# A two-block transformer kernel: the conditioning product goes to VectorE, token-major weights are joined to 512 and 384 columns, and the row-maximum scores use the whole array

## The reference, cut to what matters

```python
def hybrid_layer(x, ...):                                    # block 1
    proj = rmsnorm(x, norm1_w) @ w_in                        # 1024 x 3088
    ... y_a, y_b, y_c ...
    x = x + jnp.concatenate([y_a, y_b, y_c], -1) @ w_out
    h2 = rmsnorm(x, norm2_w)
    x = x + jnp.square(jax.nn.relu(h2 @ w_ff1)) @ w_ff2      # 1024 x 4096, 4096 x 1024

    for l in range(DEPTH_2):                                 # block 2, two layers
        mod = silu_c @ w_ada[l] + b_ada[l]                   # the conditioning product, 1024 x 6144
        sh_a, sc_a, g_a, sh_f, sc_f, g_f = jnp.split(mod[:, None, :], 6, axis=-1)
        mc = jnp.split(silu_cc @ w_ada[l][:, :n_c] + b_ada[l][:n_c], n_c // d)
        hx = rmsnorm_2(x) * (1 + sc_a) + sh_a
        ux = hx @ w_in[l]
        ...
        x = x + g_a * (jnp.concatenate([fx, ax, rx], -1) @ w_out[l])
        x = x + g_f * swiglu(rmsnorm_2(x) * (1 + sc_f) + sh_f, w_gate[l], w_up[l], w_down[l])
```

## Time and profile before

| | us |
|---|---|
| median of 3 runs | 2642.99 |
| lowest and highest | 2638.92, 2647.79 |
| span of the profiled execution | 2634.4 |
| time of the profiled execution around its span | not given; the median stands 8.6 above the span |
| PE busy in the span | 2471.9 |
| DVE, ACT, POOL busy | 870.6, 781.6, 798.1 |
| mean granted TensorE clock | 0.963 |

### The profile page before, as it was taken

The page is one execution under the profiler, slowest core; times in us unless marked ns, Lnnn a source line. Parts: engine busy times, 40 slices in busy tenths (PEclk is TensorE's granted clock), DMA queues, the critical chain, the costliest instruction groups (busy, mean ns, idle before and its releaser), DMA issues.

```text
span 2634.4 us, 37662 instructions
## 1 busy us (share of the span) xinstructions
PE 2471.9 (94%) x16546; PEld 1889.5 (72%) x16546; DVE 870.6 (33%) x1277; ACT 781.6 (30%) x980; POOL 798.1 (30%) x280
## 2 busy tenths in 40 slices
PE   7997888999999999979899999999799989999998
PEld 5874566777777787446788888888668446788886
DVE  3004236255346432842411111112442663311113
ACT  4222233122224412533322121122332543322222
POOL 3232133333333221502222222222222332344442
PEclk9997899999999999979999999999999889999999
DMA  4431023444443101002111111111210102222221
GB/s 175 172 139 33 18 84 140 162 182 152 176 160 146 48 25 47 2 3 83 62 49 64 64 65 64 64 56 49 74 49 9 47 3 103 83 103 96 96 88 56
DMA packets 41571, 216.66 MB, mean 82 GB/s; under 512 B 4088, under 2 KB 13064, under 8 KB 18112
## 3 DMA queue, kind: packets, MB, share of 16 engines
q1 hardware_dynamic: 38184, 207.87, 21.5%
...
...
## 4 chain that ended last, share of the span: by engine, by line
PE 76%; DVE 6%; ACT 3%; issue 1%; POOL 0%; DMA 0%; DVEq 0%; ACTq 0%; POOLq 0%
PE PS L676 60%; PE PS L679 3%; PE PS L1114 2%; PE PS L1147 2%; DVE s_states L1513 1%; PE PS L762 1%; DVE a_lo L599 1%; DVE tmp L606 1%; PE PS L1818 1%; PE PS L1913 1%; PE PS L1710 1%; PE PS L1164 1%; DVE x L619 1%; PE PS L1126 1%; ACT w_hi L805 1%
## 5 line engine op out<-in xcount | busy, mean ns | idle before, releaser
L2041 POOL TENSOR_TENSOR w_lo<-raw,w_hi 128x2048 fp32r<-128x2048 f32 (+3 forms) x164 | 660.8, 4034 | 1522.8 <-ACT w_hi L805 1522.8
L676 PE MATMUL PS<-a_hi,w_hi 128*128 128x512 f32 (+1 forms) x2104 | 700.1, 374 | 49.0 <-DVE a_lo L599 24.1
L676 PE MATMUL PS<-a_lo,w_hi 128*128 128x512 f32 (+1 forms) x2104 | 684.0, 366 | 0.0
L676 PE MATMUL PS<-a_hi,w_lo 128*128 128x512 f32 (+1 forms) x2104 | 680.0, 364 | 0.0
L676 PEld LDWEIGHTS PS<-a_hi,w_hi 128*128 128x128 f32 x2104 | 361.6, 190 | 149.4 <-issue 67.8
L676 PEld LDWEIGHTS PS<-a_hi,w_lo 128*128 128x128 f32 x2104 | 363.1, 190 | 68.0
L676 PEld LDWEIGHTS PS<-a_lo,w_hi 128*128 128x128 f32 x2104 | 362.5, 190 | 62.6 <-issue 1.5
L805 ACT ACTIVATE w_hi<-raw 128x2048 fp32r<-128x2048 f32 (+2 forms) x146 | 270.4, 1852 | 398.8 <-PE PS L676 185.4
L676 PE MATMUL PS<-hid_hi,w_hi 128*128 128x512 f32 (+1 forms) x784 | 260.4, 369 | 2.1 <-issue 2.1
L676 PE MATMUL PS<-hid_lo,w_hi 128*128 128x512 f32 (+1 forms) x784 | 260.8, 369 | 0.0
L676 PE MATMUL PS<-hid_hi,w_lo 128*128 128x512 f32 (+1 forms) x784 | 258.6, 366 | 0.0
...
## 6 DMA issues: line engine op xcount, KB each, us to landing
...
```

The source lines that it names most:

```text
L676: mm = p.matmul(ps[:, dst], wv[:, k, idx * P:(idx + 1) * P], av[:, k, dst], start=first, stop=last)
L2041: pool.tensor_tensor(w_lo[:, m % 2, ks, 0:ncol], raw[:, i % 3, ks, 0:ncol], w_hi[:, m % 2, ks, 0:ncol].bitcast(F32), ALU.subtract).then_in ...
```

## The change

Five things change.

1. The conditioning product. Its weights are laid transposed (`lay_turned`): on each partition one output feature, with 1024 products along the row. DVE multiplies and sums with `tensor_tensor_reduce`, which adds the bias as the start value and writes one column of `mods`: 2 x 128 features of a panel, for 2 rows of conditioning in the first 32 panels (4 instructions) and for one row in the last 16 (2 instructions). PE and ACT take no part in it any more. `c` is activated by ACT as 16 rows, stored to DRAM, and loaded back onto all partitions (`c_wide`, later `c_late`).
2. The placing of the ada panels: 12 in `in1` (after its second panel and each later one), 4 in `out1`, 8 in `ff1_0`, 8 in `ff1_1`, 12 in `ff2_0_0`, 4 in `ff2_0_1`.
3. "relu2": ACT takes ReLU from PSUM, squares and rounds; DVE only makes `hid_lo`.
4. Token-major weights are joined: two matrices of 512 columns in block 1 and one of 384 columns in each layer, each loaded as two halves of 512 rows. They stand last in their phase. A panel in memory is now contiguous in its slot (`compact`).
5. Row maxima: `k_round` holds the keys with the other head's 64 rows set to 0, so that both products of a unit use the whole array and the same query weights. For the second half of the heads it is refilled (2 roundings on ACT, 4 ticks between).

```diff
-            if n_ada < (ada_in_first if name == "in1" else len(ada)):
+            if n_ada < ada_until.get(name, 0) and (name, m) != ("in1", 0):
                 where[name].append(len(stream))
                 stream.append(ada[n_ada])
                 n_ada += 1
...
+    ada_until = {"in1": 12, "out1": 16, "ff1_0": 24, "ff1_1": ADA_BOTH, "ff2_0_0": 44, "ff2_0_1": len(ada)}
...
+        def ada_dve(v, i):
+            n = ada_rank[i]
+            _, la, c0 = stream[i]
+            v.wait_ge(s_raw[i % 3].sem, s_raw[i % 3].at(16 * (i // 3 + 1)))
+            if n == 0:
+                v.wait_ge(s_c_wide.sem, s_c_wide.at(32))
+            if n == ADA_BOTH:
+                v.wait_ge(s_c_late.sem, s_c_late.at(16))
             for m in range(PW // P):
+                w = raw[:, i % 3, 4 * m:4 * m + 4, :]
+                t = 2 * c0 + m
+                bias_ = cols[:, COLS["b_ada"][0] + la * 48 + t:COLS["b_ada"][0] + la * 48 + t + 1]
+                for c in ((1, 0) if n < ADA_BOTH else (0,)):
+                    vec = c_wide[:, 4 * c:4 * c + 4, SEQ:TOK] if n < ADA_BOTH else c_late.rearrange("p (k n) -> p k n", n=PW)
+                    products = w if c == 0 else ada_products[:] if name_of[i] == "in1" else ada_room[:, 0:4, SEQ:TOK]
+                    tell = s_ada if m == PW // P - 1 and c == 0 else v_step
+                    nc.vector.tensor_tensor_reduce(products, w, vec, 1.0, bias_, ALU.mult, ALU.add, mods[:, la, t, c:c + 1]).then_inc(tell.sem, 1)
+                    v.wait_ge(tell.sem, tell.up())
...
         def gemm_dve(v, name, l=0, norms=()):
-            late = None
-            for i in where[name] + [None]:
-                if late is not None and (i is None or stream[i][0] == "ada"):
-                    ada_dve(v, late)
-                    late = None
...
+            for i in where[name]:
                 if stream[i][0] == "ada":
+                    ada_dve(v, i)
                     continue
...
+                    if writer == "relu2":
+                        h = hid_index[n]
+                        low = local(("hid", 0), "low")
+                        nc.scalar.activation(sq[:, h % 2, span(parts)], ps[:, span(parts)], ACT.Relu).then_inc(s_rect.sem, 1)
+                        a.wait_ge(s_rect.sem, s_rect.at(h + 1))
+                        if h >= 2:
+                            a.wait_ge(low.sem, low.at(h - 1))
+                        nc.scalar.activation(tmp[:, h % 2, span(parts)], sq[:, h % 2, span(parts)], ACT.Square).then_inc(s_sqr.sem, 1)
...
+    def tok_halves(w, col, cols, tiles):
+        return [(w, 0, KT // 2, col, cols, []),
+                (w, D // 2, KT // 2, col, cols, [("tok", t, "tok", col, None) for t in tiles])]
...
-                    for h, hd in enumerate(grp["heads"]):
-                        mm = p.matmul(PS[3][:, 512 * h:512 * h + n], hd["q_r"][:, c:c + P], hd["k_r"][:, k0:k0 + n],
+                    for h in range(2):
+                        mm = p.matmul(PS[3][:, 512 * h:512 * h + n], q_round[grp["tile"] - 2][:, c:c + P], k_round[:, h, k0:k0 + n],
                                       start=True, stop=True)
```

More of the change, by code:

```diff
@@ L160, in blocks_kernel @@
     ada_rank = {i: n for n, i in enumerate(i for i, s in enumerate(stream) if s[0] == "ada")}
+    name_of = {i: name for name in order for i in where[name]}
     with ExitStack() as ctx:
@@ L387, in blocks_kernel, with compact @@
                 freed.append((s_fd, n_dve))
+        opening = {i for i in mains if not stream[i][5]}
+        def compact(buf, place, kt, ncol):
+            return buf[:, place].rearrange("p k n -> p (k n)")[:, 0:kt * ncol].rearrange("p (k n) -> p k n", n=ncol)
         slot_of, before_in = [], []
@@ L408, in slot, with opened_of @@
             return PS[slot_of[n]]
+        closed_by = {mains[rank[i] + 1]: i for i in opening}
+        halves_until = {i: n + 1 for n, i in enumerate(sorted(opening)) if stream[i][0] == "w_in_values"}
+        def opened_of(i):
+            return job_of[mains[rank[i] + 1]][0:4 if stream[i][0] == "w_in_values" else 2]
         def parts_of(parts):
@@ L673, in product @@
                         first, last = k == 0 and t == 0, k == kt - 1 and t == 2
-                        if kind == "T":
-                            for src, own, dst, c in parts_of(only or parts):
-                                mm = p.matmul(ps[:, dst], wv[:, k, idx * P:(idx + 1) * P], av[:, k, dst],
-                                              start=first, stop=last)
-                        else:
-                            mm = p.matmul(ps[:, 0:ncol], av[:, k, idx * P:(idx + 1) * P], wv[:, k, 0:ncol],
+                        for src, own, dst, c in parts_of(only or parts):
+                            mm = p.matmul(ps[:, dst], wv[:, k, idx * P:(idx + 1) * P], av[:, k, dst],
                                           start=first, stop=last)
@@ L682, in product, with half_product @@
                         mm.then_inc(s_acc.sem, 1)
-                    if only in (None, "x") and (kind == "T" or k % 4 == 3):
+                    if only in (None, "x"):
                         pass_tick(beside)
+                def half_product(n, part):
+                    ps, idx = slot(n), jobs[n][1][1]
+                    place = (m if i in opening else m - 1 + part) % 2
+                    both = [compact(buf, place, kt, ncol) for buf in (w_hi, w_lo)]
+                    for k in range(kt):
+                        for t, (wv, av) in enumerate(((both[0], b_hi), (both[0], b_lo), (both[1], b_hi))):
+                            mm = p.matmul(ps[:, 0:ncol], av[:, kt * part + k, idx * P:(idx + 1) * P], wv[:, k, :],
+                                          start=part == 0 and k == 0 and t == 0, stop=part == 1 and k == kt - 1 and t == 2)
+                    pass_tick(beside)
+                    return mm
                 def slot_free(n):
@@ L689, in slot_free @@
                         p.wait_ge(sem_.sem, count_)
+                if i in opening:
+                    for n in opened_of(i):
+                        slot_free(n)
+                        mm = half_product(n, 0)
+                    if name == "in1":
+                        mm.then_inc(s_half.sem, 1)
+                    continue
+                if jobs[job_of[i][0]][1][0] == "tok":
+                    for n in job_of[i]:
+                        if n not in opened_of(closed_by[i]):
+                            slot_free(n)
+                            half_product(n, 0)
+                        half_product(n, 1).then_inc(s_acc.sem, 1)
+                    continue
                 rising = arriving(name) if i == where[name][0] else None
@@ L820, in gemm_act @@
                 ncol = stream[i][4]
-                for n in job_of[i]:
+                for n in job_of.get(i, ()):
                     kind, idx, writer, tile, parts = jobs[n][1]
@@ L2003, in early_dve @@
                         v.wait_ge(S("rotated").sem, S("rotated").at(j + 1))
-                u, odd = divmod(tick - SCORES_AT, 2)
-                if 0 <= u < len(plan["units"]) and not odd:
+                u = unit_at(tick, l)
+                if u is not None:
                     maximum(u)
@@ L2037, in split @@
                 pieces = 4 if i in beside_norm else 1
+                low, whole, high = (compact(buf, place, kt, ncol) for buf, place in ((w_lo, m % 2), (raw, i % 3), (w_hi, m % 2)))
                 for piece in range(pieces):
```

230 lines of the change are left out of this document (103 added, 127 removed).

## The result

The changed kernel takes 2683.95 us (median of 3 runs, 2683.49 to 2685.78) against 2642.99 before: ratio 1.0147, 95% interval 1.0119 to 1.0175. It is 41 us slower; the forecast was 33 us slower, 2676, with a range of 2600 to 2715. The time of the profiled execution is now known too: 2683.49, 1.9 above its span of 2681.6.

A forecast was written before the change was run, and what follows sets the result against it. PE, with 76% of the span, was taken to bound the kernel. The terms -33.6 + 1.2 - 6 + 96 + 2 - 28.3 + 2 = +33 us gave 2676, own range 2655 to 2695, 8 in 10 from 2600 to 2715.

The forecast's parts named there:

- The release of the slot: In `out1`, `ff1_0`, `ff1_1`, loads wait for DVE's sums behind each panel: +96 us, panels of 18.0 and 16.7 us.
- a loop over two panels: In "resid" panels of `ff1`, PE's end, addition, sums, load, splits and next panel take 33.4 us for two, 16.7 each.
- `out1` and its norm: Four panels of `out1` take 57.9 us, +9; the norm waits for the last sums, +4 (+2 to +6).
- The lower bound of that stretch: `out1`, `ff1_0`, `ff1_1` without any hold of DVE by POOL and with the norm at its least: about +67 us.
- Conditioning off PE: PE gains 1.2 us per conditioning panel in `in1`, `ff1_2`, `ff1_3`, 28 panels: -33.6 us.
- Tok weights: Joined token-major weights: -11.9 us in `in1`, -8.2 in each `in2`, sum -28.3; waits for second halves' splits +2.
- Score products: Whole-array score products leave a unit at 0.37 us: 0 for 72 units, bounds -7 to +13 us.
- Scans and attention: Stages in block 1, layer 0 and layer 1: no change, 0 us in each.
- From the span to the median: The 8.6 us between profiled span and median before is carried over: span 2667.7 gives 2676.
- Rival 1: DVE's release never binds, as in `in1`, and all 48 panels gain: 2555 us; chance 0.17.
- Rival 2: The loops bind, but POOL doesn't hold the sums and the clock stays up: 2647 us; chance 0.15.
- Rival 3: The clock stays low for a whole job of each panel of the stretch: 2732 us; chance 0.08.

The follow-up runs named there:

- Run 1: Changed kernel with DVE taking the sums of each conditioning panel ahead of its jobs of the main panel (except in the first `out1` panel): 2588.56 us.
- run 3: Changed kernel with each sum in `out1`, `ff1_0` and `ff1_1` taking 256 of its 1024 products: 2623.10 us.
- run 4: Changed kernel with every split of POOL cut into 4 pieces of a quarter of the rows each: 2688.10 us.
- run 5: Changed kernel with token-major weights again as narrow panels of 1024 rows, with 256 or 128 columns, last in their phase: 2706.43 us.
- run 7: Changed kernel with the score products of the row maxima on 64 rows of the array again: 2690.32 us in a single run.
- Run 8: Both kernels profiled once more without edits: 2644.82 us for the kernel before, 2676.44 us for the changed one.
- early_spread: Changed kernel with sums ahead of the jobs and the 20 conditioning panels of `out1`, `ff1_0`, `ff1_1` spread over 36 main panels: 2560.39 us.

## Why the prediction was right

- **The release of the slot.** Right in mechanism and size: `ff1_0` and `ff1_1` +82.8 for +83.2, 18.04 for 18.0 in a relu2 panel, 16.1 to 16.8 for 16.7 in the resid panels of `ff1_0` (15.9 to 17.9 in `ff1_1`). Run 1 shows that the place of the sums causes it, run 3 that their length stands in it, run 4 and the rows of 3.48 beside POOL the hold. In the resid panels the number was luck: I had a loop over two panels, 33.4 us with 3.4 for holds and 2.0 for the clock, and the rows show a loop over one, 16.77, that goes from POOL's split through the sums and the load to the next split and has neither PE's product nor its clock in it. Run 3 agrees with the rows: 3.1 less per panel, where my loop gives 1.6.
- **`out1` and its norm.** +18.0 for +13: too small. PE's products there took 60.9 us for the 57.9 forecast, and the gap at the norm went from 8.6 to 14.8 us, 6.2 for the 4 taken, just over its upper bound.
- **The lower bound of that stretch.** "About +67" doesn't follow from its members: 8 x 17.0 + 8 x 15.0 - 194.4 + 9 is 71, and 2 for the norm makes 73. The 100.8 measured (18.0 + 82.8) lies far above both.
- **Conditioning off PE.** `ff1_2` and `ff1_3` -19.0 for 16 x 1.2 = 19.2 (before any turning), splits 10.88 us apart. `in1` gave -30.3, of it 13.0 by run 5 for the tok weights and 17 for the rest (forecast 11.9 and 14.7).
- **Tok weights.** -25.4 by run 5's stages for -28.3 + 2. In the two `in2` it was 12.4 for the 14.4 forecast. The 384-column pitch, taken at 0.173, came out at 0.173 (1070.04 to 1073.85 us, 22 matmuls); the wait for the second half's split in `in2_0` is 1.94 for the 1 taken.
- **Score products: wrong.** I took 0, bounds -7 to +13; run 7 gives -17.2. The two stages give less: they are 23.4 us shorter (13.7 + 9.7), 12.4 of it by run 5 for the weights, which leaves 11.0. Counted unit by unit in the two traces, the 72 units with the rows on either side became some 15 us shorter (in `in2_0` mostly 0.92 to 0.70 each), and part of this is lost in longer waits of PE where it turns queries and keys (2.88 for 2.12 us in `in2_0`, 8.49 for 6.69 in `in2_1`); the rest isn't accounted for. So the term is -11 to -17. The step that failed is "a unit of two 384-column matmuls takes 0.37 us, which is already what two would take one behind the other". That was true and not enough: I read the unit's own row and not the pitch of the rows ahead and behind. The 0.23 us per unit stood in the trace of the kernel before. Behind the second row comes the one below, and 946.12 - 945.66 is 0.46 where two such records are 0.35 apart without a unit between them. The rule of the Trainium skill that I weighed there ("TensorEngine Tiling (Array Packing)", "Key Properties") would have made it +13; no run here shows the parallel work, since the pair takes 0.37 with both halves. The rule that bears on it stands beside that one and I passed over it: changing the tiling mode drains the engine. The trace agrees, with 0.10 us ahead of the unit and 0.11 behind it.

```profile
946.12 0.53 PE L676 MATMUL PS<-a_lo,w_hi 128*128 128x512 f32 x2
```

- **Scans and attention.** 0 for each of the three stages; measured +2.4, +13.9 and +2.9. Run 8 shows that the middle one moves by 5 to 7 us with the clock of the execution; how much of it the change makes is open.
- **From the span to the median.** I carried over 8.6 us around the span. In the later profiled executions it is 1.7 to 1.9: the profiled execution of the kernel before was a quick one, 7 us shorter than its repetition in the stage above alone. Sum and measure are +33 and +47 by spans, +33 and +41 by medians.
- **The rivals.** Rival 1 (2555) needs a release within 1 us of the panel's end; it is what `early_spread` reaches at 2560. Rival 2 falls with the rows that POOL holds and the clock of 0.85. Rival 3 falls with 13 slow matmuls instead of a whole job.

So 2676 for 2684 was reached with two errors of opposite sign that I didn't see, -11 to -17 for the scores and +14 for one stage of scans and attention, beside a main term that was right. That they nearly cancel is luck.
